# Moving the router's weight and address arithmetic of a decoder layer from VectorE to GpSimd, with the choice of experts made by rank

## The chip, the cores and the metric

The kernel runs on one core of a Trainium2 chip. The metric is the device time of one execution in microseconds; the time before is the median of three executions. The times of single instructions come from one profiled execution, counted from the start of its span. TensorE does the matrix products, VectorE and ScalarE the elementwise work, GpSimd (POOL in the rows) small work and indirect DMAs, SyncE (SP) the other DMAs.

## What is computed

One layer of a decoder for 512 tokens of width 1024 in float32: input projection, block-sparse attention in 8 heads beside a gated linear recurrence in 8 heads, output projection, layer norm, and a hierarchical mixture of 16 experts with a second layer norm. The change touches the router of the mixture:

```python
def hier_moe(x, w_group, b_group, w_expert, b_expert, w_gate, w_up, w_down):
    ...
    g_prob = jax.nn.softmax((xt @ w_group + b_group).astype(jnp.float32), axis=-1)
    g_w, g_idx = lax.top_k(g_prob, 1)
    ...
    e_prob = jax.nn.softmax(e_logits.astype(jnp.float32), axis=-1)
    e_w, e_idx = lax.top_k(e_prob, EXPERT_TOPK)
    e_w = e_w / jnp.sum(e_w, axis=-1, keepdims=True)
    gid = g_idx[:, None] * EXPERTS_PER_GROUP + e_idx
    w_tok = g_w[:, None] * e_w
    ...
    for e in range(N_EXPERTS):
        h = jax.nn.silu(xt @ w_gate[e]) * (xt @ w_up[e])
        y = y + combine[:, e:e + 1] * (h @ w_down[e])
```

Each token has 20 logits: 4 of the groups and 4 experts in each of 4 groups. It takes the best group and in it the two best experts.

## The kernel before

The program is written engine by engine: one instruction list each for SyncE, GpSimd, TensorE, ScalarE and VectorE, kept in step by semaphores. The order in each list is the order in the source, and a waiting instruction holds up all behind it on its engine.

Tokens lie in four tiles of 128 partitions (T = 4). The first half of the program does projection, attention and recurrence; then the output projection, the layer norm and the router; then the experts, one after the other, each on the at most 128 tokens that chose it.

**Products.** Every float32 product is made of three: high part of both, high by low, low by high. ScalarE copies a unit of weights (128 partitions by 2048) from the ring of loaded units to its high part (`ehi(v)`, L1371), VectorE subtracts that from the ring to give the low part (`elo(v)`, L1801). Three such units fit (WBUF = 3). Expert 0 has units 0 to 3 (gate, gate, up, up), expert 1 starts with units 4 and 5. The ring has 12 units of 1 MB, loaded by SyncE (L429).

**Router.** After the layer norm of tile i, TensorE gives its 20 logits, and VectorE puts them into `r_l` (`logits_of`, L1833). When the last tile's are there, `first_max` finds in each group of four the largest and turns it into a one-hot, breaking ties by weights 4, 3, 2, 1 (L1866 to L1870, five instructions); it runs for groups and experts together, and once more for the second expert. The mask of chosen experts (`r_msk`, L1879) goes to TensorE, which counts with two kinds of matmul (L1039, L1041) the place of each token in its expert's list. VectorE turns places into one-hots of slots (`place(e)`, L1895), TensorE multiplies them by token numbers (`placed(e)`, L1048), and VectorE copies the result to `first` (`slots_of`, L1901): the tokens of experts 0 to 3 (EARLY = 4). GpSimd gathers their rows from HBM by it (`gather(e)`, L585); TensorE transposes them (L1118 for expert 0, L1063 for the others).

**Weights and records.** Behind the slots of experts 0 and 1 VectorE makes what later experts need: the differences of logits (L1908 to L1911), which ScalarE takes the exponential of (L1401), the address of each token's record (L1914 to L1918, semaphore `s_addr`), and the weights (L1920 to L1924). GpSimd then scatters eight groups of records to HBM (`scatter_record`, L591), with `gather(2)` behind the fifth and `gather(3)` behind the seventh, reads the full table back (L610) and goes on with the gathers and added rows of the other experts (L617). `gather(2)` fills the buffer that expert 0 used, and the transposes of expert 2 wait for it.

**Fillers.** `keep_warm(n, b)` issues n matmuls on constants whose result nobody reads (L677).

## Time and profile before

| | |
|---|---|
| median of three executions | 617.22 us (616.98 to 617.65) |
| profiled execution, its own time | 616.78 us |
| its span, first to last instruction | 614.9 us |
| TensorE busy | 593.7 us, 97% of the span, 3691 matmuls |
| VectorE busy | 478.1 us, 78% |
| ScalarE busy | 373.9 us, 61% |
| GpSimd busy | 128.2 us, 21%, 111 instructions |
| DMA | 155.77 MB, mean 253 GB/s |

Busy shares are means over the whole program. The chain of waits leads back from the last instruction through whatever released each step; its shares say which engine set the end. A timeline row gives an instruction's start, its duration, and in brackets how long the engine stood idle before it and which engine and line ended that. Row groups that merge equal instructions give a count (x2) and the time from the first's start to the last's end.

### The profile page before, as it was taken

The page shows a single profiled execution, that of the slowest core. Times are in us where ns is not written, and L with a number is a line of the kernel's source. Part 1 is how long each engine was busy: PE and PEld are TensorE (multiplying, and loading weights), DVE is VectorE, ACT ScalarE, POOL GpSimd, SP SyncE. Part 2 cuts the span into 40 slices and gives each one's busy share as a digit, 9 for nine tenths or more (in the row PEclk, how much of TensorE's full clock was granted, in tenths as well). Part 3 has the DMA queues.
Part 4 walks back from the last instruction along what each step waited for, and adds up shares of the span by engine and source line. Part 5 has one row for each costly group of instructions (what it writes and reads, how often), then busy time and mean ns, then how long its engine had stood idle before and what let it go on. Part 6 is the DMA issues. An engine that isn't in the chain of part 4 may idle for free.

```text
span 614.9 us, 9763 instructions
## 1 busy us (share of the span) xinstructions
PE 593.7 (97%) x3691; PEld 478.3 (78%) x3691; DVE 478.1 (78%) x572; ACT 373.9 (61%) x401; POOL 128.2 (21%) x111
## 2 busy tenths in 40 slices
PE   8999999999999999999799999999999999999991
PEld 7878888788888678877688888888888888888880
DVE  3758598794577775446898889888888988888967
ACT  3659434431215984213478877877877777787745
POOL 0004222290000441000484532111110111111010
PEclk9999999999999999999899999999999999999996
DMA  8831233223306002975699999999999999999754
GB/s 325 298 96 60 62 131 114 90 72 78 72 1 205 2 3 102 422 278 225 211 388 419 419 373 366 391 388 394 412 399 390 389 390 388 399 411 395 267 172 136
DMA packets 42573, 155.77 MB, mean 253 GB/s; under 512 B 11955, under 2 KB 12163, under 8 KB 30252
## 3 DMA queue, kind: packets, MB, share of 16 engines
q1 hardware_dynamic: 37516, 138.40, 57.7%
q0 software_dynamic: 5024, 16.92, 10.6%
q8 instruction: 23, 0.38, 0.3%
q14 instruction: 10, 0.08, 0.0%
HBM read 139.96 MB, written 15.34 MB: 253 GB/s over the span
## 4 chain that ended last, share of the span: by engine, by line
PE 92%; DVE 4%; ACT 1%; issue 1%; DMA 1%; DVEq 0%; SPq 0%
PE psum L663 26%; PE psum L665 25%; PE psum L664 25%; PE psum L1063 2%; PE psum L781 2%; PE psum L921 2%; PE psum L898 2%; PE psum L1080 1%; PE psum L885 1%; PE psum L677 1%; DMA cst<-in_c_main 1%; ACT ring L1338 1%; PE psum L823 1%; PE psum L811 1%; PE psum L767 1%
## 5 line engine op out<-in xcount | busy, mean ns | idle before, releaser
L1801 DVE TENSOR_TENSOR w_lo<-ring,w_hi 128x2048 fp32r<-128x2048 f32 x95 | 216.4, 2294 | 23.7 <-ACT w_hi L1371 23.6
L663 PE MATMUL psum<-w_hi,act_hi 128*128 128x512 f32 x538 | 216.5, 402 | 0.8 <-DVE w_lo L1801 0.6
L665 PE MATMUL psum<-w_hi,act_lo 128*128 128x512 f32 x538 | 210.2, 391 | 0.0
L664 PE MATMUL psum<-w_lo,act_hi 128*128 128x512 f32 x538 | 209.9, 390 | 0.0
L1371 ACT ACTIVATE w_hi<-ring 128x2048 fp32r<-128x2048 f32 x96 | 182.1, 1916 | 25.0 <-PE psum L665 22.4
L663 PEld LDWEIGHTS psum<-w_hi,act_hi 128*128 128x128 f32 x538 | 101.2, 188 | 27.0 <-DVE w_lo L1801 4.7
L665 PEld LDWEIGHTS psum<-w_hi,act_lo 128*128 128x128 f32 x538 | 101.0, 188 | 21.8
L664 PEld LDWEIGHTS psum<-w_lo,act_hi 128*128 128x128 f32 x538 | 101.2, 188 | 19.1
L617 POOL DMA_INDIRECT acc_dram<-misc,slots x15 | 25.4, 1693 | 193.7 <-ACT misc L1421 175.9
L1219 ACT ACTIVATE w_hi<-ring 128x2048 fp32r<-128x2048 f32 x17 | 32.6, 1918 | 49.2 <-PE psum L665 47.4
L1530 DVE TENSOR_TENSOR w_lo<-ring,w_hi 128x2048 fp32r<-128x2048 f32 x17 | 39.8, 2344 | 22.3 <-ACT w_hi L1219 22.1
L663 PE MATMUL psum<-act_hi,w_hi 128*128 128x512 f32 x128 | 50.9, 398 | 0.4 <-DVE w_lo L1549 0.4
L664 PE MATMUL psum<-act_lo,w_hi 128*128 128x512 f32 x128 | 49.9, 390 | 0.0
L665 PE MATMUL psum<-act_hi,w_lo 128*128 128x512 f32 x128 | 49.9, 390 | 0.0
L1601 DVE TENSOR_TENSOR misc<-ring 64x256 f32<-64x256 f32 x48 | 34.8, 725 | 1.1
L551 POOL TENSOR_TENSOR ring<-ring 128x2048 f32<-128x2048 f32 x6 | 22.6, 3765 | 54.4 <-PE psum L781 44.8
L575 POOL TENSOR_SCALAR misc<-cst,small 128x64 f32<-128x64 f32 x32 | 14.8, 477 | 80.0 <-DVE small L1732 79.9
L663 PEld LDWEIGHTS psum<-act_hi,w_hi 128*128 128x128 f32 x128 | 24.0, 188 | 6.0 <-issue 0.8
L665 PEld LDWEIGHTS psum<-act_hi,w_lo 128*128 128x128 f32 x128 | 24.0, 188 | 5.1
L664 PEld LDWEIGHTS psum<-act_lo,w_hi 128*128 128x128 f32 x128 | 24.1, 188 | 4.7
L1413 ACT ACTIVATE act_hi<-psum 128x512 fp32r<-128x512 f32 x16 | 9.6, 600 | 25.7 <-PE psum L1080 25.7
L1935 DVE TENSOR_TENSOR act_lo<-psum,act_hi 128x1024 fp32r<-128x1024 f32 x15 | 18.4, 1226 | 7.8 <-ACT act_hi L1405 7.7
(254 smaller groups left out, 697.0 us busy)
## 6 DMA issues: line engine op xcount, KB each, us to landing
ring<-in_w_gate SPq DMA_DIRECT2D x32, 1024.0 KB, 17.3
ring<-in_w_up SPq DMA_DIRECT2D x32, 1024.0 KB, 19.1
ring<-in_w_down SPq DMA_DIRECT2D x32, 1024.0 KB, 19.6
ring<-in_w_in SPq DMA_DIRECT2D x13, 1024.0 KB, 6.2
ring<-in_w_o SPq DMA_DIRECT2D x4, 1024.0 KB, 4.8
acc_dram<-ring SPq DMA_DIRECT2D x5, 512.0 KB, 4.0
ring<-in_x SPq DMA_DIRECT2D x2, 1024.0 KB, 6.5
ring<-strip_dram SPq DMA_DIRECT2D x8, 256.0 KB, 4.7
```

Source lines behind the costliest of these rows:

```text
L551: pool.tensor_tensor(wlev[l].rearrange("p a (n s) -> p (a n) s", s=2 * m), src, src[:, :, m - 1:m].broadcast_to((P, SEQ * PAIRS // (2 * m) ...
L575: pool.tensor_scalar(wide[:, n // (2 * T) % 2, i, 64 * (h % 2):64 * (h % 2) + 64], ones[:, 0:64], prec[:, col:col + 1], None, ALU.mult).th ...
L617: pool.indirect_dma_start(out=acc_dram, out_offset=bass.IndirectOffsetOnAxis(ap=index.bitcast(U32), axis=0), in_=yb[:, b, :], in_offset=No ...
L663: pe.matmul(dst, lh, rh, start=first, stop=False, skip_group_check=True)
L664: pe.matmul(dst, lh, rl, start=False, stop=False, skip_group_check=True)
L665: return pe.matmul(dst, ll, rh, start=False, stop=last, skip_group_check=True)
L1219: act.activation(w_hi[:, u % WBUF, :], ring[:, u % MIX_RING, :], ACT.Copy).then_inc(s_hi, 1)
L1371: act.activation(w_hi[:, v0 % WBUF, :], ring[:, slot, :], ACT.Copy).then_inc(s_hi, 1)
L1530: dve.tensor_tensor(w_lo[:, u % WBUF, :], ring[:, u % MIX_RING, :], w_hi[:, u % WBUF, :].bitcast(F32), ALU.subtract).then_inc(s_lo, 1)
L1601: dve.tensor_tensor(qz[rows, a, :, par, :].rearrange("p c (n t) -> p c n t", t=m), right(wlev[l]), right(hq), ALU.mult).then_inc(s_qz, 1)
L1801: dve.tensor_tensor(w_lo[:, v0 % WBUF, :], ring[:, slot, :], w_hi[:, v0 % WBUF, :].bitcast(F32), ALU.subtract).then_inc(s_lo, 1)
L1935: dve.tensor_tensor(e_lo[:, b, :], banks(0, 2), e_hi[:, b, :].bitcast(F32), ALU.subtract).then_inc(s_etlo, 1)
```

## The change

The five-instruction `first_max`, run twice, is replaced by ranks. `ranks(t0)` subtracts in each four every logit from every other (128 partitions by 160 for two tiles), compares the differences with a table of zeros and smallest numbers that settles ties, and sums: 0 is the largest, 1 the second. For tiles 0 and 1 it stands ahead of the last tile's residual, for tiles 2 and 3 behind the last logits. The mask then takes one comparison and one fused comparison and product.

GpSimd makes the differences, one-hots, addresses and the sum behind the weights, in 25 instructions that each wait for the one before (`then`), where sums over 16 are halved four times (`folded`). VectorE keeps the reciprocal, which now stands behind `place(3)` and ahead of `elo(3)` and waits for `s_addr` 1; one product goes back to GpSimd behind it, ahead of the record scatters. ScalarE's exponential stands behind `ehi(3)`, not behind `ehi(2)`, and waits for GpSimd. `elo(1)` stands right behind `elo(0)`. TensorE's fillers are 29, 9 and 30 instead of 32, 0 and 24, and the first unit's products come in the order high by high, high by low, low by high for all four blocks. The constants have 16 numbers for the ties in place of 4, and the experts' numbers are shifted by 16.

```diff
+            pool.wait_ge(s_rneed, 1)
+            pooled[0] = 4
+            pool.wait_ge(s_pool, 4)
+            then(pool.tensor_tensor(r_x[:, :, 0:NG], r_l[:, :, 0:NG], r_top.broadcast_to((P, T, NG)), ALU.subtract))
+            then(pool.tensor_scalar(r_hot, r_rank[:, :, NG:NL], 0.5, None, ALU.is_lt))
+            then(pool.tensor_scalar(r_hot2, r_rank[:, :, NG:NL], 1.0, None, ALU.is_equal))
+            then(pool.tensor_tensor(four(r_sel[:, 0]), four(r_hot), group_four, ALU.mult))
+            then(pool.tensor_tensor(four(r_sel[:, 1]), four(r_hot2), group_four, ALU.mult))
+            then(pool.tensor_tensor(r_step, r_sel[:, 1], r_sel[:, 0], ALU.subtract))
+            then(pool.tensor_tensor(r_step, r_step, r_l[:, :, NG:NL], ALU.mult))
+            folded(lambda a, b: r_step[:, :, a:b], NE, ALU.add)
+            pool.tensor_copy(r_x[:, :, NG:NG + 1], r_step[:, :, 0:1]).then_inc(s_rneed, 1)
...
+            then(pool.tensor_scalar(r_pos, r_at1, float(NE), None, ALU.mult))
+            then(pool.tensor_tensor(r_pos, r_pos, e16.broadcast_to((P, T, NE)), ALU.add))
+            for k in range(2):
+                then(pool.tensor_tensor(r_sel[:, k], r_sel[:, k], r_pos, ALU.mult))
...
+            folded(lambda a, b: sel[:, :, a:b], NE, ALU.add)
+            then(pool.tensor_copy(addr_i[:, :, :].rearrange("p k i -> p (k i)").rearrange("p (n a) -> p n a", a=1), sel[:, :, 0:1]))
+            pool.wait_ge(s_rexp, 1)
+            folded(lambda a, b: r_x[:, :, a:b], NG, ALU.add)
+            then(pool.tensor_scalar(r_q, r_x[:, :, NG:NG + 1], ALPHA, ALPHA, ALU.mult, ALU.add))
+            pool.tensor_tensor(r_gsum, r_x[:, :, 0:1], r_q, ALU.mult).then_inc(s_addr, 1)
+
             pool.wait_ge(s_pads, 16 * (SEQ // P))
             pool.wait_ge(s_addr, 2)
+            then(pool.tensor_tensor(weight_of(rec_i[:, :, 1, 2:3]), weight_of(rec_i[:, :, 0, 2:3]), r_x[:, :, NG:NG + 1], ALU.mult))
             for n in range(2 * T):
...
-            keep_warm(32, 4)
+            keep_warm(29, 4)
...
             last.then_inc(s_pos, 1)
+            keep_warm(9, 1)
             pe.wait_ge(s_rec, 1)
...
-            keep_warm(24, 1)
+            keep_warm(30, 1)
...
-            act.wait_ge(s_rneed, 1)
-            act.activation(r_x, r_x, ACT.Exp).then_inc(s_rexp, 1)
...
             ehi(3, 0)
+            act.wait_ge(s_rneed, 2)
+            act.activation(r_x, r_x, ACT.Exp).then_inc(s_rexp, 1)
             ehi(4, 0)
...
+            def ranks(t0):
+
+                ls = r_l[:, t0:t0 + 2, :].rearrange("p t (g e) -> p (t g) e", e=4)
+                shape = (P, 2 * (1 + NG), 4, 4)
+                link(dve.tensor_tensor(r_beats, ls.rearrange("p s (a i) -> p s a i", a=1).broadcast_to(shape),
+                                       ls.rearrange("p s (j a) -> p s j a", a=1).broadcast_to(shape), ALU.subtract))
...
+                link(dve.tensor_tensor(r_beats, r_beats, tie.broadcast_to(shape), ALU.is_ge))
+                link(dve.tensor_reduce(r_rank[:, t0:t0 + 2, :].rearrange("p t (g e a) -> p (t g) e a", e=4, a=1), r_beats, AX.X, ALU.add))
+
+            ranks(0)
             residual(T - 1, 1)
...
             link(logits_of(T - 1))
...
-            first_max(r_l, r_hot, r_top, r_first, T * (1 + NG))
...
-            first_max(r_l2, r_hot2, r_top2, r_first2, T * NG)
...
+            ranks(T // 2)
+            link(dve.tensor_scalar(r_group, r_rank[:, :, 0:NG], 0.5, None, ALU.is_lt))
+
+            dve.scalar_tensor_tensor(out=four(r_msk), in0=four(r_rank[:, :, NG:NL]), scalar=1.5, in1=group_four,
+                                     op0=ALU.is_lt, op1=ALU.mult).then_inc(s_mask, 1)
...
             elo(0, 0)
+            elo(1, 0)
...
-            elo(1, 0)
             elo(2, 0)
             place(2)
             place(3)
+            dve.wait_ge(s_addr, 1)
+            dve.reciprocal(weight_of(rec_i[:, :, 0, 2:3]), r_gsum).then_inc(s_addr, 1)
             elo(3, 0)
```

The order of the instructions on VectorE, from the slots of experts 0 and 1 (`first`) to the fourth unit's low part, before. L1801 is `elo`, L1895 `place`, L1960 and L1962 the low part of expert 0's rows:

```order
L1901 CAST first<-psum 128x2 x2
L1908 TENSOR_TENSOR misc<-misc 128x4x4
L1909 TENSOR_TENSOR misc<-misc 128x16
...
L1923 RECIPROCAL rec_i<-misc 128x4
L1924 TENSOR_TENSOR rec_i<-rec_i,misc 128x4
L1801 TENSOR_TENSOR w_lo<-ring,w_hi 128x2048
L1960 TENSOR_TENSOR act_lo<-psum,act_hi 128x512
L1962 TENSOR_TENSOR act_lo<-psum,act_hi 128x512
L1801 TENSOR_TENSOR w_lo<-ring,w_hi 128x2048 x2
L1895 TENSOR_TENSOR act_hi<-cst,misc 128x512
L1895 TENSOR_TENSOR act_lo<-cst,misc 128x512
L1801 TENSOR_TENSOR w_lo<-ring,w_hi 128x2048
```

And now, with the line numbers of the changed kernel (L1848 is `elo`, L1934 `place`):

```order
L1940 CAST first<-psum 128x2 x2
L1848 TENSOR_TENSOR w_lo<-ring,w_hi 128x2048 x2
L1982 TENSOR_TENSOR act_lo<-psum,act_hi 128x512
L1984 TENSOR_TENSOR act_lo<-psum,act_hi 128x512
L1848 TENSOR_TENSOR w_lo<-ring,w_hi 128x2048
L1934 TENSOR_TENSOR act_hi<-cst,misc 128x512
L1934 TENSOR_TENSOR act_lo<-cst,misc 128x512
L1989 RECIPROCAL rec_i<-misc 128x4
L1848 TENSOR_TENSOR w_lo<-ring,w_hi 128x2048
```

The small instructions are gone, the second unit's low part stands ahead of expert 0's rows, and the reciprocal stands ahead of the fourth unit's.

On GpSimd, from the gathers of experts 0 and 1 to those of 2 and 3, before:

```order
L585 DMA misc<-x_dram,first 128x1024 x2
L591 DMA slot_dram<-rec_i,addr_i 8192x3 x5
L585 DMA misc<-x_dram,first 128x1024
L591 DMA slot_dram<-rec_i,addr_i 8192x3 x2
L585 DMA misc<-x_dram,first 128x1024
```

And now (L589 is the gather, L595 the scatter, L616 a halving):

```order
L589 DMA misc<-x_dram,first 128x1024 x2
L621 TENSOR_TENSOR misc<-misc 128x4x4
L622 TENSOR_SCALAR misc<-misc 128x64
...
L629 COPY misc<-misc 128x4
L632 TENSOR_SCALAR misc<-misc 128x64
...
L638 CAST addr_i<-misc 128x8
...
L642 TENSOR_TENSOR misc<-misc 128x4
L646 TENSOR_TENSOR rec_i<-rec_i,misc 128x4
L595 DMA slot_dram<-rec_i,addr_i 8192x3 x5
L589 DMA misc<-x_dram,first 128x1024
```

26 instructions stand between the second gather and the first scatter, and the third gather is still behind five scatters.

## Rows read from the trace of the kernel before

**Rows 1.** The page, part 4: chain of waits, shares by engine.

```profile
PE 92%; DVE 4%; ACT 1%; issue 1%; DMA 1%; DVEq 0%; SPq 0%
```

**Rows 2.** Timeline of TensorE, 285 to 350: start us, us, instruction, tile, count [idle before].

```profile
290.67 3.65 PE L677 MATMUL psum<-cst 128*128 128x256 bf16 x32
295.88 0.25 PE L1039 MATMUL psum<-msk_b,ones_b 128*128 128x64 bf16 x4 [1.56 <-DVE msk_b L1879]
...
298.37 4.46 PE L677 MATMUL psum<-cst 128*128 128x256 bf16 x24
302.67 1.16 PE L1118 MATMUL psum<-cst,misc 128*128 128x128 f32 x8
...
307.69 0.47 PE L663 MATMUL psum<-w_hi,act_hi 128*128 128x512 f32 x1 [0.59 <-DVE w_lo L1801]
...
329.67 1.04 PE L1063 MATMUL psum<-cst,misc 128*128 128x128 f32 x8
```

**Rows 3.** Busy time by stretch: us, PE, PEld, DVE, ACT, POOL; granted clock; DMA.

```profile
299.00:300.00 1.00, 1.00 (x6) 0.70 (x5) 0.90 (x6) 0.22 (x1) 0.70 (x2) 0.50 0.00 0
```

**Rows 4.** Timeline of VectorE, 285 to 350.

```profile
287.51 0.69 DVE L1820 SCALAR_TENSOR_TENSOR ring<-ring,psum 128x512 f32<-128x512 f32 x1 [3.89 <-PE psum L665]
...
292.34 0.24 DVE L1866 TENSOR_REDUCE misc<-misc 128x20 f32<-128x80 f32 x1
...
295.51 0.22 DVE L1879 TENSOR_TENSOR msk_b<-misc 128x64 bf16<-128x64 f32 x1
...
301.53 2.29 DVE L1801 TENSOR_TENSOR w_lo<-ring,w_hi 128x2048 fp32r<-128x2048 f32 x1
...
305.26 4.48 DVE L1801 TENSOR_TENSOR w_lo<-ring,w_hi 128x2048 fp32r<-128x2048 f32 x2
...
310.86 2.29 DVE L1801 TENSOR_TENSOR w_lo<-ring,w_hi 128x2048 fp32r<-128x2048 f32 x1
...
315.23 2.29 DVE L1801 TENSOR_TENSOR w_lo<-ring,w_hi 128x2048 fp32r<-128x2048 f32 x1
```

**Rows 5.** Line 585 (row gather) alone, 298 to 299: issue to landing.

```profile
DMA to landing us min/median/max: 4.2/4.2/4.2
```

**Rows 6.** Line 442 (last quarter written to HBM) alone, 291 to 293.

```profile
L442 SPq DMA_DIRECT2D x_dram<-ring x1: 320/320/320, 292.2 to 292.2; - x1
...
DMA to landing us min/median/max: 2.9/2.9/2.9
```

**Rows 7.** Timeline of GpSimd, 285 to 400: gathers (L585) and record scatters (L591).

```profile
298.45 1.05 POOL L585 DMA_INDIRECT misc<-x_dram,first  x1 [64.55 <-DVE first L1901]
...
302.47 2.24 POOL L591 DMA_INDIRECT slot_dram<-rec_i,addr_i  x1 [1.69 <-DVE rec_i L1924]
305.01 0.98 POOL L591 DMA_INDIRECT slot_dram<-rec_i,addr_i  x1 [0.30 <-issue]
...
310.89 3.10 POOL L591 DMA_INDIRECT slot_dram<-rec_i,addr_i  x1 [0.30 <-issue]
315.58 2.79 POOL L585 DMA_INDIRECT misc<-x_dram,first  x1 [1.59 <-DVE first L1901]
```

**Rows 8.** Timeline of GpSimd, small operations elsewhere in the program.

```profile
135.67 0.39 POOL L560 CAST rec_i<-cst 128x24 int32<-128x24 f32 x1
136.00 0.29 POOL L561 CAST tri_b<-cst 128x128 bf16<-128x128 f32 x1
...
341.90 0.18 POOL L614 COPY small<-slots 128x1 f32<-128x1 f32 x1 [5.49 <-DMA slots<-slot_dram]
```

**Rows 9.** The page, part 5: GpSimd operation on 64 elements, the nearest in size.

```profile
L575 POOL TENSOR_SCALAR misc<-cst,small 128x64 f32<-128x64 f32 x32 | 14.8, 477 | 80.0 <-DVE small L1732 79.9
```

**Rows 10.** Timeline of ScalarE, 285 to 360.

```profile
295.78 1.28 ACT L1401 ACT_TABLE_LOAD   x1
...
307.19 1.92 ACT L1371 ACTIVATE w_hi<-ring 128x2048 fp32r<-128x2048 f32 x1 [2.68 <-PE psum L1129]
```

**Rows 11.** Line 585 alone, 315 to 316: issue to landing.

```profile
DMA to landing us min/median/max: 10.6/10.6/10.6
```

More of the change, by code:

```diff
@@ L66 @@
 C_SCAN = C_MASK + 64 * (1 + len(LEVELS))
-C_W4 = C_SCAN + SEQ
-C_E16 = C_W4 + 4
+C_TIE = C_SCAN + SEQ
+C_E16 = C_TIE + 16
 C_REC = C_E16 + NE
@@ L87, in shape_constants @@
     c[:, C_SCAN:C_SCAN + SEQ] = (np.arange(SEQ) % CH != 0)[None]
-    c[:, C_W4:C_W4 + 4] = [4, 3, 2, 1]
-    c[:, C_E16:C_E16 + NE] = np.arange(NE)
+    c[:, C_TIE:C_TIE + 16] = [0 if i < j else np.finfo(np.float32).tiny for j in range(4) for i in range(4)]
+    c[:, C_E16:C_E16 + NE] = np.arange(NE) - NE
     for i in range(T):
@@ L297, in build, with four @@
         r_msk = msk_b[:, :].rearrange("p (i e) -> p i e", i=T)
-        r_l, r_hot, r_top, r_first = rcol(T, NL), rcol(T, NL), rcol(T * (1 + NG), 1), rcol(T * (1 + NG), 1)
-        r_l2, r_hot2, r_top2, r_first2 = rcol(T, NE), rcol(T, NE), rcol(T * NG, 1), rcol(T * NG, 1)
-        r_x, r_d, r_both, r_gsum, r_gw, r_q = rcol(T, NG + 1), rcol(T, NG), rcol(T, NE), rcol(T, 1), rcol(T, 1), rcol(T, 1)
+        r_l, r_group, r_hot, r_hot2, r_top = rcol(T, NL), rcol(T, NG), rcol(T, NE), rcol(T, NE), rcol(T, 1)
+        r_rank, r_beats, r_step = rcol(T, NL), rcol(2 * (1 + NG), 4, 4), rcol(T, NE)
+        r_x, r_gsum, r_q = rcol(T, NG + 1), rcol(T, 1), rcol(T, 1)
+        def four(v):
+            return v.rearrange("p t (g e) -> p t g e", g=NG)
+        group_four = r_group.rearrange("p t (g a) -> p t g a", a=1).broadcast_to((P, T, NG, EPG))
         r_sel, r_pos, r_t16, r_at1, r_adr, r_cnt = rcol(2, T, NE), rcol(T, NE), rcol(2 * T, NE), rcol(T, NE), rcol(2 * T, 1), rcol(1)
@@ L598, in _, with then, folded @@
             gather(1)
+            pooled = [2]
+            def then(ins):
+                pooled[0] += 1
+                ins.then_inc(s_pool, 1)
+                pool.wait_ge(s_pool, pooled[0])
+            def folded(v, n, op):
+                while n > 1:
+                    n //= 2
+                    then(pool.tensor_tensor(v(0, n), v(0, n), v(n, 2 * n), op))
+            pool.wait_ge(s_rneed, 1)
+            pooled[0] = 4
+            pool.wait_ge(s_pool, 4)
+            then(pool.tensor_tensor(r_x[:, :, 0:NG], r_l[:, :, 0:NG], r_top.broadcast_to((P, T, NG)), ALU.subtract))
@@ new lines, in _ @@
+            folded(lambda a, b: r_step[:, :, a:b], NE, ALU.add)
+            pool.tensor_copy(r_x[:, :, NG:NG + 1], r_step[:, :, 0:1]).then_inc(s_rneed, 1)
+            e16 = cst[:, C_E16:C_E16 + NE].rearrange("p (a e) -> p a e", a=1)
+            then(pool.tensor_scalar(r_pos, r_at1, float(NE), None, ALU.mult))
+            then(pool.tensor_tensor(r_pos, r_pos, e16.broadcast_to((P, T, NE)), ALU.add))
+            for k in range(2):
+                then(pool.tensor_tensor(r_sel[:, k], r_sel[:, k], r_pos, ALU.mult))
@@ new lines, in _ @@
+            sel = r_sel.rearrange("p k i e -> p (k i) e")
+            folded(lambda a, b: sel[:, :, a:b], NE, ALU.add)
[4 more added lines that the diff above has]
+            pool.tensor_tensor(r_gsum, r_x[:, :, 0:1], r_q, ALU.mult).then_inc(s_addr, 1)
@@ L1120, in _ @@
             pe.wait_ge(s_x1tsb, T + 2)
-            pe.wait_ge(s_lo, MIX_UNITS + 1)
-            block = lambda k: (slice(k * P, (k + 1) * P), slice(k * DE, (k + 1) * DE))
-            for k in range(4):
-                xs, ws = block(k)
-                high(bank(2), e_hi[:, 0, xs], w_hi[:, 0, ws], w_lo[:, 0, ws], k == 0)
-            pe.wait_ge(s_xtlofirst, 1)
-            for k in range(4):
-                xs, ws = block(k)
-                last = pe.matmul(bank(2), e_lo[:, 0, xs], w_hi[:, 0, ws], start=False, stop=False, skip_group_check=True)
+            pe.wait_ge(s_hi, MIX_UNITS + 1)
+            passes = [(e_hi, w_hi), (e_hi, w_lo), (e_lo, w_hi)]
+            for n, (x, w) in enumerate(passes):
+                if n == 1:
+                    pe.wait_ge(s_lo, MIX_UNITS + 1)
+                elif n == 2:
+                    pe.wait_ge(s_xtlofirst, 1)
+                for k in range(4):
+                    last = pe.matmul(bank(2), x[:, 0, k * P:(k + 1) * P], w[:, 0, k * DE:(k + 1) * DE], start=(n == 0 and k == 0), stop=False,
+                                     skip_group_check=True)
             last.then_inc(s_used, 1)
@@ L1885, in _ @@
             dve.wait_ge(s_mask, 1)
+            dve.tensor_reduce(r_top, r_l[:, :, 0:NG], AX.X, ALU.max)
             dve.wait_ge(s_pos, 1)
             pos = psum[:, 7, 0:T * NE].rearrange("p (i e) -> p i e", i=T)
-            e16 = cst[:, C_E16:C_E16 + NE].rearrange("p (a e) -> p a e", a=1)
-            link(dve.scalar_tensor_tensor(out=r_at1, in0=pos, scalar=1.0, in1=r_msk, op0=ALU.add, op1=ALU.mult))
+            dve.scalar_tensor_tensor(out=r_at1, in0=pos, scalar=1.0, in1=r_msk, op0=ALU.add, op1=ALU.mult).then_inc(s_rneed, 1)
+            dve.wait_ge(s_rneed, 1)
             def place(e):
```

36 lines of the change are left out of this document (1 added, 35 removed).

## The prediction

> **What bounds the kernel now.** I read the chain of waits first: TensorE carries 92% of the span [rows 1]. In the expert half it never starves for long; the largest holes are around the router, where a token's choice of experts must become an index before the first rows can be gathered. The timeline of TensorE shows them [rows 2]: it waits 1.56 us for the choice mask (295.88), fills time with 24 dummy matmuls (298.37, 4.46 us), transposes expert 0's rows at 302.67, waits 0.59 us for the low part of the second weight unit (307.69), and transposes expert 2's rows at 329.67. From there on the experts run on TensorE's own pace. So a change here is worth what it moves the transpose at 329.67, if nothing behind it is hurt. The 24 dummies are slow: 32 others took 3.65 us (114 ns each), these 186 ns each, since the granted clock is 0.50 at 299 to 300 [rows 2, 3], the lower level (1.2 GHz), after TensorE had done little since the first dummies ended at 294.3.
>
> **The choice.** VectorE starts twelve instructions in a row at 292.34 and the mask at 295.51 [rows 4]: 3.17 us, 0.264 each. The change leaves three on 160 elements, one on 16, and the mask. From 0.24 us for 80 elements and 2.29 for 2048 [rows 4] an element costs 1.04 ns, so 160 cost 0.32, with the 0.03 between starts 0.35; three are 1.05, the small one 0.2. The mask starts at 293.6 instead of 295.5: **1.9 us earlier**. The same three for tokens 0 to 255 lie ahead of the wait for TensorE that ends at 287.51 after 3.89 us idle [rows 4], which covers their 1.05; without it they would cost 1.05.
>
> **TensorE's fillers.** 29 dummies from 290.67 last 3.3 us, to 294.0, when the mask's matmuls can start. Nine more (1.0 us) bridge to the one-hot matmuls. The clock should not fall, so the 30 dummies ahead of expert 0 last 3.4 us, from 296.5 to 299.9. Expert 0's gather started at 298.45, released by VectorE's slots [rows 7], and landed 4.2 later [rows 5], just as the old dummies ended. It moves to 296.55. The HBM rows that it reads were issued at 292.2 and landed 2.9 later [rows 6], so they don't hold it. It lands at 300.75: the transposes come 1.9 earlier. The new order of the twelve first products (four with low weights moved behind four with high) issues as many matmuls: nothing, since both low parts are there by then.
>
> **Low weights.** VectorE loses 15 small instructions between the slots and 301.53 and runs two low-part subtractions there instead of one, so the 0.59 wait at 307.69 goes [rows 2]: 0.6 more. Together 2.5 us; at best the transpose of 329.67 would come at 327.2.
>
> **What GpSimd takes over.** 25 instructions in one chain, each waiting for the one before, until the first weight sum (s_addr 1), and one product after VectorE's reciprocal. Nothing in the trace is such a chain. The nearest rows: a copy of one element 0.18 and two casts that start 0.33 apart [rows 8], and 0.44 to 0.48 for 64 elements with an operand per partition [rows 9]. Bounds are 0.18 and 0.44 per step; I take 0.33, as most steps have 4 to 64 elements. GpSimd also yields to VectorE. A record scatter takes 0.98 (305.01), but 2.24 when it starts inside the subtraction of 301.53 to 303.82, and 3.10 inside that of 310.86 to 313.15 [rows 4, 7]: both end 0.85 to 0.9 behind the subtraction's end. So a GpSimd instruction issued into a subtraction of two SBUF tensors waits for its end. The Trainium skill (SBUF — State Buffer, Who interferes with whom) says the same, that such an instruction and a GpSimd one that reads SBUF exclude each other for the whole instruction; but by it the first to issue wins, so a GpSimd step would also hold a subtraction up, by at most its 0.3. The trace has no case that I could price.
> By these rows: the second gather waits for the first subtraction (right behind the slots, 296.7 to 299.0) and ends at 299.9; the chain starts at 301.3 behind the second. Until the third (from 305.26, less 1.9: 303.4 to 305.7) some 6 steps pass, 3 at the edges of it and of the two one-hots, to 307.0. There VectorE waits for the chain and leaves GpSimd alone: 16 steps of 0.33 end at **312.3** (bounds 309.4 and 314.5; the lower one is set by ScalarE, below).
> The Trainium skill (GPSIMD Engine Reference, Engine selection) advises VectorE for such elementwise work, GpSimd being about twice slower for two inputs. By it a 0.2 us step would be 0.4, and the chain end at 313.8; that is inside the bounds.
>
> **The exponential.** ScalarE's copy at 307.19 moves to 305.3, ends at 307.2, then comes the table load of 1.28 [rows 10] and the exponential, 308.6 at the earliest; the last four steps of GpSimd's chain follow it. The 12 steps that it waits for are then done (9 by 307.0, three more by 308.0). Its next copy is held up 0.3, which VectorE's wait covers.
>
> **VectorE waits, first effect.** Behind the new wait stand the low part of the fourth unit, expert 1's low part, the slots of experts 2 and 3, and the low part of the fifth. Before, the fourth ran at 310.86 and the fifth at 315.23 to 317.52 [rows 4], just ahead of TensorE. Now the fourth starts at 312.6, ends at 314.9; with the same distance at most (2.1) or the work alone (1.4) the fifth ends at 318.6 to 319.3: TensorE would be 1.1 to 1.8 us later than before, take 1.4.
>
> **GpSimd's queue, second effect, and the larger one.** The eight record scatters and the gather of expert 2, which stands behind five of them, are queued behind the chain. Before, the scatters started at 302.47, the fifth ended at 313.99, and the gather started at 315.58 [rows 7]. Now: wait at 312.3, reciprocal, then the last product, which meets the fourth subtraction and waits until 314.9; scatters from 315.3. Five took 11.5 us where each met a subtraction, and would take 6.4 alone (0.98 and 0.30 between); VectorE has rather fewer subtractions per us in that stretch, so I take 10. The gather starts at 325.6, **10.0 later** (bounds: 318.7 and 329.2). It needed 10.6 us to land [rows 11], since the weight loads fill the DMA engines, against 4.2 on an idle queue [rows 5]. It lands at 336.2. Before, it landed at 326.2 and was needed at 329.67: slack of 3.5. So TensorE transposes expert 2 at 336.2, **6.5 later than before**; this swallows both the 2.5 won and the 1.4 lost. In a wait of over 4 us the clock should fall again: the old fall cost 4.46 less 24 times 0.114, or 1.7 us [rows 2]; bounds 0 and 1.7, I take 0.9, as I don't know how much falls into the wait itself.
> Sum: 6.5 and 0.9 make 7.4. The profiled execution took 616.78, 0.44 under the median 617.22. On the median: **624.6**.
>
> **Rivals.**
> *A, VectorE's wait alone.* The gather lands in time because it moves faster, and only the first effect stays: 617.2 and 1.4, 618.6 (617.0 to 619.2). For it: a gather on an idle queue takes 4.2. Against: the loads are just as dense there.
> *B, faster.* GpSimd's steps cost under 0.2, the scatters slip between subtractions (6.4), and the gather started at 318.7 lands, even after 8.5 us, before 327.2: then 2.5 are won, 614.7, less up to 0.5 of the fifth unit's low part. It decides at a gather start of about 317 with 10.6 to land, or 323 with 4.2. For it: the exponential is due just as the steps would then be done. Against: even with free steps the last product meets the fourth subtraction, and scatters did meet one each.
> *C, the queue is later still.* The slots' table, read behind all eight scatters, is late for expert 1's output weight and for the added rows, and ScalarE waits too: 629 or more. Before, it came in at 341.9 [rows 8]; 10 us later is near what the next output can stand.
> *That the choice does not shorten*: the ranks' broadcasts could run slower, up to 0.5 each; this takes 0.5 from the 1.9 and nothing from the forecast, since the gather of expert 2 sets it.
>
> **How the numbers follow.** Forecast 0.60, its own range 620.5 to 628.5 (gather start 2.5 us either way, clock 0 to 1.7); A 0.13, half of it within 0.2% (1.2 us, about what a measurement tells from no change); B 0.17; C 0.10. Faster 0.17, same 0.06, slower 0.77. The range from 615.0 to 628.5 leaves out C and half of B.
>
> **What would show it.** The mask at 293.6; no 0.50 clock at 299; GpSimd's chain from 301 to about 312 with VectorE idle before the reciprocal; the gather of expert 2 starting near 325 and TensorE idle over 4 us ahead of expert 2's transposes. I am wrong if that gather lands before TensorE asks for it, or if the chain is done by 309.

## The result and the profile after

Before 617.1 us (median of four executions, 616.85 to 617.65), changed 624.18 us (median of four, 623.39 to 628.72); ratio 1.0124, 95% interval 1.0098 to 1.0149. The changed kernel is slower by 1.2%. The forecast was 624.6. The median of 624.18 lies between 623.42 and 624.94, and the four executions spread over 5.3 us. The changed kernel's profiled execution took 623.39 with a span of 621.6, against 616.78 and 614.9: 6.7 us more of span.

TensorE's share of the chain of waits fell from 92 to 88% [rows 1], and GpSimd's, not among the shares before, is 4%:

```profile
PE 88%; DVE 4%; POOL 4%; issue 2%; DMA 1%; ACT 0%; DVEq 0%; POOLq 0%
```

The chain itself, from 312 to 338 us (start, us, what), is the view that settles where the time went. It leaves TensorE and runs through GpSimd's queue:

```profile
312.34 0.21 POOL misc L642
...
312.58 0.19 DVE rec_i L1989
...
312.90 2.12 POOL rec_i L646
...
315.31 0.07 POOL slot_dram L595
...
316.70 2.50 POOL slot_dram L595
...
323.44 2.23 POOL slot_dram L595
...
325.97 8.36 DMA misc<-x_dram,first
...
334.37 1.97 PE psum L1109 x8
```

GpSimd's last sum (L642), VectorE's reciprocal (L1989), the product that waits inside a subtraction (L646, 2.1 us), five record scatters (L595, from 315.31 to 325.67; three are shown), the gather of expert 2 in flight for 8.4 us, and only then TensorE's transposes at 334.37, where they stood at 329.67 before [rows 2].

TensorE, timeline, 285 to 350:

```profile
290.88 3.33 PE L722 MATMUL psum<-cst 128*128 128x256 bf16 x29
...
296.61 3.45 PE L722 MATMUL psum<-cst 128*128 128x256 bf16 x30
300.99 1.16 PE L1164 MATMUL psum<-cst,misc 128*128 128x128 f32 x8 [0.93 <-DMA misc<-x_dram,first]
...
307.97 1.04 PE L1109 MATMUL psum<-cst,misc 128*128 128x128 f32 x8
...
315.00 0.79 PE L708 MATMUL psum<-w_hi,act_hi 128*128 128x512 f32 x1 [2.45 <-DVE w_lo L1848]
...
334.37 1.97 PE L1109 MATMUL psum<-cst,misc 128*128 128x128 f32 x8 [2.31 <-DMA misc<-x_dram,first]
```

The front works as meant. The whole execution is 0.2 us later when the router begins. The 30 dummies take 3.45 us (115 ns each) where 24 took 4.46, expert 0's transposes come at 300.99 instead of 302.67, and expert 1's at 307.97 instead of 310.53. At the fourth unit TensorE waits 2.45 us, at expert 2 2.31 us.

VectorE, timeline, 285 to 350:

```profile
287.72 0.69 DVE L1867 SCALAR_TENSOR_TENSOR ring<-ring,psum 128x512 f32<-128x512 f32 x1 [2.82 <-PE psum L710]
...
293.83 0.22 DVE L1920 SCALAR_TENSOR_TENSOR msk_b<-misc 128x64 bf16<-128x64 f32 x1
...
303.58 2.28 DVE L1848 TENSOR_TENSOR w_lo<-ring,w_hi 128x2048 fp32r<-128x2048 f32 x1
305.78 0.81 DVE L1934 TENSOR_TENSOR act_hi<-cst,misc 128x512 fp32r<-128x512 f32 x1
...
312.58 0.18 DVE L1989 RECIPROCAL rec_i<-misc 128x4 f32<-128x4 f32 x1 [5.33 <-POOL misc L642]
312.67 2.28 DVE L1848 TENSOR_TENSOR w_lo<-ring,w_hi 128x2048 fp32r<-128x2048 f32 x1
...
322.54 2.29 DVE L1848 TENSOR_TENSOR w_lo<-ring,w_hi 128x2048 fp32r<-128x2048 f32 x1 [0.91 <-ACT w_hi L1418]
```

The wait that ended at 287.51 after 3.89 us idle [rows 4] is now 2.82: the ranks of the first two tiles lie in it. The mask starts at 293.83. Before the reciprocal at 312.58 VectorE stands idle for 5.33 us, and the fourth subtraction (L1848) follows it, and then the fifth at 316.07.

GpSimd, timeline, some of the 25 steps:

```profile
303.23 0.33 POOL L626 TENSOR_TENSOR misc<-misc 128x64 f32<-128x64 f32 x1
303.63 2.42 POOL L627 TENSOR_TENSOR misc<-misc 128x64 f32<-128x64 f32 x1
306.12 1.77 POOL L616 TENSOR_TENSOR misc<-misc 128x32 f32<-128x32 f32 x4
...
309.91 1.23 POOL L616 TENSOR_TENSOR misc<-misc 128x64 f32<-128x64 f32 x4
...
312.90 2.11 POOL L646 TENSOR_TENSOR rec_i<-rec_i,misc 128x4 f32<-128x4 f32 x1 [0.36 <-DVE rec_i L1989]
```

The step at 303.23 takes 0.33 us; the next, the same operation on the same size, takes 2.42, since it starts inside the subtraction of 303.58 to 305.86. The four halvings at 306.12 beside the one-hots take 1.77, those at 309.91 with VectorE idle 1.23.

ScalarE, timeline: the exponential comes as early as its table load lets it.

```profile
307.44 1.28 ACT L1497 ACT_TABLE_LOAD   x1
308.73 0.22 ACT L1497 ACTIVATE misc<-misc 128x20 f32<-128x20 f32 x1
```

Granted clock by stretch (us; busy PE, PEld, DVE, ACT, POOL; clock; DMA share, GB/s):

```profile
296.00:300.00 4.00, 4.00 (x36) 3.45 (x36) 3.46 (x5) 0.00 (x0) 3.01 (x2) 1.00 0.72 256
314.00:320.00 6.00, 5.00 (x12) 3.93 (x13) 5.93 (x8) 1.38 (x1) 5.10 (x4) 0.50 1.00 422
334.00:338.00 4.00, 3.63 (x13) 3.27 (x14) 0.56 (x1) 1.62 (x2) 1.52 (x2) 0.57 0.99 405
```

At 296 to 300 the clock is full; before, it was 0.50 at 299 to 300 [rows 3]. It is 0.50 from 314 to 320, from within the wait at the fourth unit on, and again for much of 334 to 338, behind the wait for expert 2's rows.

### The profile page after: what moved, and what is told of

The parts are those of the page before. It is cut to its first block, busy times and chain, and to the rows that moved or that the text cites. A ratio compares the mean times of both kernels' runs of the same rounds, so it can differ in the third digit from the quotient of the medians.

```text
span 621.6 us, 9796 instructions
## 1 busy us (share of the span) xinstructions
PE 598.1 (96%) x3703; PEld 482.6 (78%) x3703; DVE 475.8 (77%) x554; ACT 374.0 (60%) x401; POOL 137.7 (22%) x137
## 4 chain that ended last, share of the span: by engine, by line
PE 88%; DVE 4%; POOL 4%; issue 2%; DMA 1%; ACT 0%; DVEq 0%; POOLq 0%
PE psum L708 24%; PE psum L710 23%; PE psum L709 23%; PE psum L1109 2%; PE psum L826 2%; PE psum L943 2%; PE psum L966 2%; PE psum L722 2%; PE psum L930 2%; DMA misc<-x_dram,first 1%; POOL slot_dram L595 1%; PE psum L1126 1%; PE psum L868 1%; PE psum L856 1%; PE psum L1003 1%
## 5 line engine op out<-in xcount | busy, mean ns | idle before, releaser
L1848 DVE TENSOR_TENSOR w_lo<-ring,w_hi 128x2048 fp32r<-128x2048 f32 x95 | 216.9, 2298 | 25.2 <-ACT w_hi L1418 23.9
```

The costliest lines, as they stand in the source:

```text
L1848: dve.tensor_tensor(w_lo[:, v0 % WBUF, :], ring[:, slot, :], w_hi[:, v0 % WBUF, :].bitcast(F32), ALU.subtract).then_inc(s_lo, 1)
```

## The experiments

Two theories stood against each other. **The queue:** the records and, behind five of them, expert 2's gather leave GpSimd too late; all else is swallowed by TensorE's wait for that gather. **The wait:** VectorE's idle time ahead of the reciprocal, with the half clock behind it, is what costs. Each run is compared with executions of the kernel before on the same chip, whose medians were 617.32 to 617.77 us; so two runs are compared by their ratios, not by their times.

**1. The gather second in the queue.**

```diff
             for n in range(2 * T):
-                if n == 5:
+                if n == 1:
                     pool.wait_ge(s_slots, 3)
                     gather(2)
```

> The changed kernel with the gather of expert 2 behind the first record scatter instead of the fifth. Queue theory (the gather's place in GpSimd's queue sets TensorE's restart at expert 2): the gather starts near 316.7 us, lands by 327, TensorE no longer waits for it (2.3 us) and its clock does not fall a second time (1.7 us): 4.0 us faster than the changed kernel, about 620. Rival (VectorE's wait for GpSimd's sum, with the half clock behind it, is all that costs): no change, 623.4 to 624.2.

Measured: 622.37 us, ratio 1.0091 (1.0061 to 1.0122); 620.69 in the profiled execution. The gather started at 316.27 and TensorE's wait at expert 2 was gone (transposes at 330.43), but only some 2 us of 4 came back: the ratio fell from 1.0124 to 1.0091, with intervals that overlap, so that the profile says more here than the time. GpSimd's and ScalarE's timelines show why:

```profile
316.27 2.51 POOL L589 DMA_INDIRECT misc<-x_dram,first  x1 [0.30 <-issue]
...
348.67 1.50 POOL L659 COPY small<-slots 128x1 f32<-128x1 f32 x1 [5.03 <-DMA slots<-slot_dram]
```

```profile
350.26 1.12 ACT L1466 ACTIVATE misc<-psum,small 128x1024 f32<-128x1024 f32 x1 [2.47 <-POOL small L659]
```

The table of records, read back behind all eight scatters, gives expert 1's output weight (L659). It came at 348.67, ScalarE's output (L1466) waited 2.47 us for it, and TensorE 1.61 behind that. The gather was the first thing to be late; the table is the next.

**2. The same, and TensorE kept busy at the fourth unit.**

```diff
+            keep_warm(22, 4)
             in_unit(3, 0, 1, 3, 0)
             step(1, 0)
```

> As the run before, and 22 dummy matmuls on TensorE ahead of expert 0's fourth unit, where it waits for VectorE. If the 0.50 clock from 313.9 to 320.7 us comes from that wait, it is gone, and a further 2.8 us (half of the 5.7 us that TensorE works in it): about 617. If the clock falls for another reason: as the run before, about 620.

Measured: 622.42 us, ratio 1.0067 (1.0048 to 1.0086). The 22 dummies ran in 2.58 us and the granted clock is 1.00 over 312 to 322, so the half clock at 314 to 320 goes with the idle time at the fourth unit; that such idle time does not always bring it is seen in run 9, where TensorE waited 2.63 us and kept the full clock. The time was not that of the expectation, 617, but that of run 1:

```profile
312.54 2.58 PE L722 MATMUL psum<-cst 128*128 128x256 bf16 x22
```

```profile
ACT misc L1467 <- POOL small L659: 4.0, 1, 4.0
...
PE psum L708 <- DVE w_lo L1849: 3.1, 1, 3.1
```

(the second fence: engine and line waited for, us in total, times, longest.) Little was won in front. In run 1 the lower clock lasted only 3.4 us, a loss of 1.7 and not of 2.8; here TensorE waited 0.6 us for VectorE right behind (at 318.59 and 321.78), this execution began its router 0.5 us later, and expert 2's transposes came at 330.56, against 330.43 in run 1. Of the ten scatters and gathers ahead of the table one more took over 1.8 us, the ten took 2.9 us longer in all, the table came at 351.64, 3 us later than in run 1, and TensorE waited 3.1 us in one go behind it. The little that was won in front was more than paid at the table.

**3. Rank alone.** The weights and addresses go back to VectorE, to their old place; ranks, fillers and the order of the first unit's products stay.

```diff
-            then(pool.tensor_tensor(r_x[:, :, 0:NG], r_l[:, :, 0:NG], r_top.broadcast_to((P, T, NG)), ALU.subtract))
...
+            link(dve.tensor_tensor(r_x[:, :, 0:NG], r_l[:, :, 0:NG], r_top.broadcast_to((P, T, NG)), ALU.subtract))
+            dve.tensor_scalar(r_hot, r_rank[:, :, NG:NL], 0.5, None, ALU.is_lt)
...
             elo(0, 0)
-            elo(1, 0)
```

> Only the choice by rank and the fillers are kept: weights and addresses are made on VectorE again, where they were before, 17 instructions, and the exponential stands where it was. Queue theory: gather of expert 2 in time, mask 1.9 us earlier, low part of the second unit late by up to 0.9: 615 to 615.7, faster than before by 1.5 to 2. Rival (the ranks or fillers themselves cost): 617 or more.

Measured: 615.67 us (ten executions), ratio 0.9968 (0.9958 to 0.9978): faster than both kernels. TensorE's timeline:

```profile
301.37 1.16 PE L1123 MATMUL psum<-cst,misc 128*128 128x128 f32 x8 [1.39 <-DMA misc<-x_dram,first]
...
306.39 0.47 PE L667 MATMUL psum<-w_hi,act_hi 128*128 128x512 f32 x1 [0.60 <-DVE w_lo L1807]
...
328.37 1.04 PE L1068 MATMUL psum<-cst,misc 128*128 128x128 f32 x8
```

Transposes of expert 0 at 301.37 and of expert 2 at 328.37, the wait for the second unit's low part still there at 0.60. So the choice by rank does what it says, and the loss comes with the move to GpSimd and the order on VectorE that goes with it. The two profiled executions differ by 0.8 us of span only (614.1 against 614.9); where the rest of the 2 us between the medians lies is not shown. A repetition beside other runs (eleventh run):

> The run with rank alone and weights on VectorE once more, beside the other two on one chip: 615.7, 0.2 to 0.4% under the kernel before.

gave 615.66, ratio 0.9972 (0.9960 to 0.9984).

**4. The mechanism alone, in the kernel before.** Nothing of the change; only the two gathers behind all scatters.

```diff
             for n in range(2 * T):
-                if n == 5:
-                    pool.wait_ge(s_slots, 3)
-                    gather(2)
                 if n == 7:
-                    gather(3)
+                    pool.wait_ge(s_slots, 3)
                 scatter_record(n)
+            gather(2)
+            gather(3)
```

> The kernel before with the gathers of experts 2 and 3 behind all eight record scatters; nothing else. Queue theory: the gather of expert 2 starts near 321.5 us instead of 315.6, lands near 332, TensorE waits 2.4 us for it and may lose up to 1.7 at half clock: 619.5 to 621. Rival (a late gather is made good by an emptier queue or by slack): 617.1, no change.

Measured: 621.05 us, ratio 1.0048 (1.0031 to 1.0065). GpSimd's first scatter and gather, and TensorE's transposes:

```profile
303.60 2.23 POOL L591 DMA_INDIRECT slot_dram<-rec_i,addr_i  x1 [1.88 <-DVE rec_i L1923]
...
322.92 2.51 POOL L585 DMA_INDIRECT misc<-x_dram,first  x1 [0.30 <-issue]
```

```profile
333.03 1.16 PE L1062 MATMUL psum<-cst,misc 128*128 128x128 f32 x8 [1.64 <-DMA misc<-x_dram,first]
```

The gather started at 322.92, TensorE waited 1.64 us for it. Late gathers alone make the kernel slower, by 3 us (0.48%). The profiled execution is longer than that of before by 4.7 us of span, and not all of this is the gather: expert 1's transposes, which stand ahead of it, came 1.6 us late already (312.10 against 310.53), as this execution had the lower clock from 297 to 305 (before: 298 to 302). Another 1.8 arise by expert 2's transposes, and 1.1 by those of expert 3.

**5. The old fillers in the changed kernel.**

```diff
-            keep_warm(29, 4)
+            keep_warm(32, 4)
...
-            keep_warm(9, 1)
...
-            keep_warm(30, 1)
+            keep_warm(24, 1)
```

> The changed kernel with TensorE's fillers as before (32, none, 24). Queue theory: the front of the router is swallowed by the wait for expert 2's gather, so nothing changes in the time (within 0.5 us of the changed kernel, 4 to 7 above the kernel before), though the clock is 0.50 near 297 to 300 us again. Rival (the fillers win or cost something in the end): a difference over 1 us.

Measured: 628.62 us, ratio 1.0164 (1.0107 to 1.0220), the four executions 623.33, 627.90, 629.33 and 630.41. The expectation failed as to the size, though the interval overlaps that of the changed kernel (1.0098 to 1.0149), so that a cost of the old fillers is not shown. It failed as to the clock, too: the 24 fillers took 2.79 us at the full clock. The profile shows how fine the balance is. The chain on GpSimd and the first three scatters stand where they do in the changed kernel, to 0.1 us. Then:

```profile
315.31 1.08 POOL L595 DMA_INDIRECT slot_dram<-rec_i,addr_i  x1 [0.29 <-POOL rec_i L646]
...
322.16 2.62 POOL L595 DMA_INDIRECT slot_dram<-rec_i,addr_i  x1 [0.31 <-issue]
...
326.35 2.13 POOL L589 DMA_INDIRECT misc<-x_dram,first  x1 [0.30 <-issue]
```

The fourth scatter met a subtraction (2.62 us, against 0.96 in the changed kernel), so did the gather (2.13 against 1.00). It landed at 336.6, 2.3 later, TensorE waited 5.64 us, and there the clock was at its lower level for 6.8 us instead of 3.4. What tipped it was the start of one subtraction on VectorE:

```profile
321.66 2.29 DVE L1847 TENSOR_TENSOR w_lo<-ring,w_hi 128x2048 fp32r<-128x2048 f32 x1
```

In the changed kernel it started at 322.54, behind 0.91 us of waiting for ScalarE and 0.4 us behind the start of the fourth scatter; here it started 0.5 us ahead of the scatter, with no wait before it. The likely reason is that the lower clock at the fourth unit lasted 3.4 us here and 6.8 there, so that TensorE gave ScalarE and VectorE their next work sooner. The changed kernel's own executions spread over 5 us in the same way. That each of them is such a slip is argued from these two profiles, not shown.

**6. VectorE's wait moved back.**

```diff
-            dve.wait_ge(s_addr, 1)
-            dve.reciprocal(weight_of(rec_i[:, :, 0, 2:3]), r_gsum).then_inc(s_addr, 1)
             elo(3, 0)
             xt_lo(1, 1)
             slots_of(2, EARLY, 6)
             elo(4, 0)
+            dve.wait_ge(s_addr, 1)
+            dve.reciprocal(weight_of(rec_i[:, :, 0, 2:3]), r_gsum).then_inc(s_addr, 1)
```

> The changed kernel with VectorE's wait and reciprocal behind the fifth unit's low part instead of ahead of the fourth's. VectorE no longer idles over 5 us, TensorE no longer waits 2.45 us at the fourth unit. Queue theory: the scatters start at most 0.8 us later, so the gather of expert 2 lands at 334.5 to 335.5 all the same and the time is that of the changed kernel, 623.5 to 625. Rival (VectorE's wait costs by itself): 2 to 4 us faster than the changed kernel.

Measured: 630.74 us, ratio 1.0214 (1.0197 to 1.0231): **slower** than the changed kernel by 6 us, though TensorE's wait at the fourth unit was gone. It waited 1.28 us for the fifth unit instead, kept the full clock up to there, and was ready for expert 2 at 328.54, 3.5 us sooner than in the changed kernel (332.06). That was all lost in the wait for the gather, 11.3 us: the wait theory is dead as an account of the time. The queue theory is right on what sets the time, but had expected no later gather. GpSimd's timeline:

```profile
317.19 2.71 POOL L595 DMA_INDIRECT slot_dram<-rec_i,addr_i  x1 [0.55 <-POOL rec_i L646]
...
328.56 2.42 POOL L595 DMA_INDIRECT slot_dram<-rec_i,addr_i  x1 [0.30 <-issue]
331.29 1.00 POOL L589 DMA_INDIRECT misc<-x_dram,first  x1 [0.30 <-issue]
```

Five scatters took from 317.19 to 330.98, 13.8 us, where they took 10.4 in the changed kernel: VectorE is idle for only 0.9 us in all between 317 and 330, and each of the five takes over 2 us. They also began 1.9 us later, not 0.8 as expected: GpSimd's four halvings met the fourth subtraction, which now ran beside them (3.69 us, against 1.77), and the last product waited 2.4 us for the reciprocal. The gather started 5.3 us later than in the changed kernel, expert 2's transposes came at 339.81, and the clock stayed low long after (second and third column of numbers: us and TensorE busy):

```profile
332.00:340.00 8.00, 0.20 (x1) 0.20 (x2) 0.00 (x0) 0.00 (x0) 4.19 (x5) 0.51 1.00 408
340.00:346.00 6.00, 6.00 (x19) 5.04 (x19) 2.56 (x2) 2.82 (x2) 2.35 (x4) 0.51 0.06 17
```

From 339.8 to 345.9 TensorE worked at half clock, a loss of 3.0 us; with the 10.1 us by which the transposes are late that makes 13.1 of the 13.2 us of span over the kernel before.

**7. Both waits taken out.** The reciprocal as in run 6, and expert 2's gather ahead of all scatters.

```diff
+            pool.wait_ge(s_slots, 3)
+            gather(2)
             pool.wait_ge(s_pads, 16 * (SEQ // P))
             pool.wait_ge(s_addr, 2)
...
-                if n == 5:
-                    pool.wait_ge(s_slots, 3)
-                    gather(2)
```

> The reciprocal behind the fifth unit's low part and the gather of expert 2 ahead of all record scatters. Both waits of the changed kernel are gone, expert 2's transposes come at 327 to 327.5 us. If the records' table is the third in the row: it comes at 348 to 349 us, 3 us after TensorE's pace would need expert 1's weight, and ScalarE's output of expert 1 waits for it; with the clock's fall 618.5 to 620.5. If nothing else is late: 615.

Measured: 625.53 us, ratio 1.0121 (1.0101 to 1.0140). TensorE did not wait for expert 2's rows, but reached them at 330.08 and not at 327: it waited 1.28 us for the fifth unit, and in this execution the first 29 fillers took 4.99 us instead of 3.33, at the lower clock for the most part. And the table took over as the bound, by more than expected: it came at 353.85.

```profile
PE psum L707 <- DVE w_lo L1847: 7.1, 2, 5.8
...
ACT misc L1465 <- POOL small L658: 6.7, 1, 6.7
```

ScalarE waited 6.7 us for GpSimd's weight, TensorE 5.8 us in one go behind it. The table comes 7 to 13 us later than with rank alone (341.0 in run 3, 347.8 in the changed kernel, 353.9 here): in these runs, moving work about in the queue only chose who is late.

**8. Rank alone with the old fillers.**

> The run with rank alone and weights on VectorE, with TensorE's fillers as before (32, none, 24). If only the choice wins the time: the 24 slow fillers (4.5 us from 296.6) end at 301, as the gather lands at 300.8, and the time is that of rank alone, 615.7. If the clock kept up by the new fillers is part of it: about 1 us slower, 616.5 or more.

(the edit is that of run 5, on the kernel of run 3.) Measured: 616.68 us (ten executions, 615.52 to 617.79), ratio 0.9986 (0.9976 to 0.9997), against 0.9968 with the new fillers (0.9958 to 0.9978, so that the intervals just touch). Its profiled execution took 615.68, as fast as run 3's, and the 24 fillers ran at the full clock, 2.79 us, with TensorE idle for 1.13 and 1.49 us around them. So in this execution, as in run 5, the earlier mask alone kept the clock up, without the nine fillers between. What the slower half of its executions did no profile shows. By the medians the fillers are worth about 1 us, and how stays open.

**9. The last product on VectorE.**

```diff
-            dve.reciprocal(weight_of(rec_i[:, :, 0, 2:3]), r_gsum).then_inc(s_addr, 1)
+            link(dve.reciprocal(weight_of(rec_i[:, :, 0, 2:3]), r_gsum))
+            dve.tensor_tensor(weight_of(rec_i[:, :, 1, 2:3]), weight_of(rec_i[:, :, 0, 2:3]), r_x[:, :, NG:NG + 1], ALU.mult).then_inc(s_addr, 1)
```

> The changed kernel with the last product on VectorE behind the reciprocal, so that GpSimd's queue holds nothing but scatters when the sum is done. The product ran 2.1 us on GpSimd, of which 1.9 was the fourth subtraction. If the block by subtractions sets the queue, the first scatter now meets the same subtraction: it ends near 316.0 instead of 316.4 us, and the time stays within 1.5 us of the changed kernel (622.5 to 625.5). If the product itself was the cost: expert 2's gather 2 us earlier, 620 to 621.

Measured: 626.73 us, ratio 1.0134 (1.0114 to 1.0154). The time is above the expected stretch, but the ratio cannot be told from the changed kernel's 1.0124 (1.0098 to 1.0149). That the product was the cost, 620 to 621, is refuted. The first scatter met the fourth subtraction as foreseen (ended at 316.00), and each of the next four took over 2 us, too:

```profile
313.70 2.30 POOL L595 DMA_INDIRECT slot_dram<-rec_i,addr_i  x1 [1.28 <-DVE rec_i L1989]
...
325.06 3.06 POOL L595 DMA_INDIRECT slot_dram<-rec_i,addr_i  x1 [0.30 <-issue]
328.43 2.07 POOL L589 DMA_INDIRECT misc<-x_dram,first  x1 [0.30 <-issue]
```

Five took 14.4 us and the gather started at 328.43. In this execution the clock did not fall at the fourth unit, and VectorE's subtractions came closer together: one started at 321.64, with no wait before it. In the changed kernel the same one waited 0.91 us for ScalarE and started at 322.54, and one scatter slipped through. The reading, argued from these profiles and that of run 5, is that the loss on TensorE paid a part of itself back on GpSimd.

**10. Rank alone, weights later.** To take the 0.60 us left in run 3, the first subtraction goes ahead of the address chain and the five weight instructions behind the second; expert 2's gather goes out behind three scatters instead of five.

```diff
             for n in range(2 * T):
-                if n == 5:
+                if n == 3:
...
+            elo(0, 0)
             link(dve.tensor_tensor(r_x[:, :, 0:NG], r_l[:, :, 0:NG], r_top.broadcast_to((P, T, NG)), ALU.subtract))
...
-            dve.wait_ge(s_rexp, 1)
-            link(dve.tensor_reduce(r_gsum, r_x[:, :, 0:NG], AX.X, ALU.add))
...
-            elo(0, 0)
...
             elo(1, 0)
+            dve.wait_ge(s_rexp, 1)
+            link(dve.tensor_reduce(r_gsum, r_x[:, :, 0:NG], AX.X, ALU.add))
...
```

> Rank alone with weights on VectorE, but the first subtraction ahead of the address chain, the five weight instructions behind the second subtraction, and expert 2's gather behind three scatters. It takes the 0.60 us wait for the second unit's low part. If the records' table has the slack that the trace shows (it is read at 341.0 us, needed at 346.5), it gains 0.6 us on rank alone. If scatters that start 5 us later make the table late again: 1 to 3 us slower than rank alone.

Measured: 616.79 us, ratio 0.9989 (0.9975 to 1.0002). The wait for the second unit's low part stayed, at 0.59. In that order the second subtraction (at 304.97, 2.28 us) stands behind expert 0's two low parts, the last of which starts at 304.37, and VectorE even stood idle for 0.61 us ahead of them: it is not a full VectorE that TensorE waits for there, but this order. The table came at 346.01, 5 us later than in run 3, 1 of which this execution had lost by expert 1's transposes. The median shows no gain, and run 3 stays the best version. What the profiled execution lost, it lost ahead of the edit: its first 29 fillers ran at the lower clock for the most part,

```profile
290.80 4.99 PE L681 MATMUL psum<-cst 128*128 128x256 bf16 x29
```

4.99 us for the 29 against 3.33 in run 3. From expert 1's transposes to the end it took 304.6 us, run 3 304.9. So the later table cost nothing in it, and whether the slower median comes from the edit or from more executions with such a start is not shown.

## Why the prediction was right

The time forecast was 624.6 and is 624.18; the mechanism and nearly every time up to the gather's start are those of the forecast: GpSimd's chain holds up its queue, the gather of expert 2 starts 10 us late, TensorE waits for it, and both what was won in front and what the fourth unit cost are swallowed. That the time agrees within 0.4 us is luck. Two terms behind the gather's start are off by 1.8 and 0.8 us and partly cancel, the profiled execution lies 0.8 under the median, and the executions spread over more than 5 us. Step by step, predicted and measured on the profiled execution:

| step | predicted | measured |
|---|---|---|
| mask starts | 293.6 | 293.83, with all 0.2 later |
| expert 0's transposes | 300.8 | 300.99 |
| won up to expert 1's transposes | 2.5 us | 2.56 us |
| exponential | 308.6 | 308.73 |
| GpSimd's sum done | 312.3 | 312.54 |
| first scatter | 315.3 | 315.31 |
| five scatters | 10 us | 10.4 us |
| expert 2's gather starts | 325.6 | 325.97 |
| it lands | 336.2 | 334.33 |
| expert 2's transposes, later by | 6.5 us | 4.7 us |
| half clock behind them | 0.9 us | 1.7 us |
| TensorE idle ahead of expert 2 | over 4 us | 2.31 us |
| span, longer by | 7.4 us | 6.7 us |

Two terms were mis-sized against each other. **The landing:** taken as 10.6 us from its issue [rows 11], it was 8.4. The gather of [rows 11] itself took 2.79 us on GpSimd, as it started inside a subtraction [rows 4, 7]; the new one took 1.00, which accounts for 1.8 of the 2.2 us. I had carried that block over into a place where I had not looked whether a subtraction stood. **The clock:** I took half of 1.7 us; the 3.4 us at the lower level began as TensorE resumed (334.4), so all of it was paid. The 4.7 and 1.7 us make 6.4 of the 6.7 of span; the other 0.3 is not traced.

**One sign did not come.** The prediction named TensorE idle over 4 us ahead of expert 2's transposes. It was 2.31, because the gather landed 1.9 us earlier than forecast and TensorE itself came 1.0 later than the 331.1 that the forecast implies (329.67 and 1.4).

**A second fall was missed.** The wait at the fourth unit was foreseen, its clock was not: TensorE worked at half speed from 315.0 to 320.7, 2.8 us. Rival A, priced at 1.4, would have been 2.4: TensorE stood ready for expert 2 at 332.06, against 329.67. It added nothing to the time at expert 2, as the gather came later still, which is what run 6 confirms from the other side.

**The clock in front.** The prediction put the full clock of the 30 fillers down to the fillers ahead of them. Runs 5 and 8 had it without them, so the earlier mask, which left TensorE less idle time, was enough in their profiled executions.

**The steps of GpSimd.** 0.33 was the estimate; 24 steps from 301.53 to 312.54, less 2.1 us in which one stood inside a subtraction and 0.5 beside the one-hots, make 0.35 each. (The prediction's working by a step of 0.4 us, 307.0 and 16 steps, gives 313.4 and not 313.8. Its range, by the terms it names, would be 621.2 to 627.9, a little narrower than stated. Neither touches the forecast.) The rule of the Trainium skill (SBUF — State Buffer, Who interferes with whom), that a VectorE instruction with two SBUF inputs and a GpSimd one that reads SBUF exclude each other, agrees with the trace in one direction: the step of 2.42 us above. In the other it fits VectorE's one-hots, which took 0.81 and 0.74 beside GpSimd's steps against 0.69 and 0.68 before; this direction, which the trace of before could not price, is worth 0.18 us in all. The Trainium skill's advice to give elementwise work on a tile to VectorE and not to GpSimd (GPSIMD Engine Reference, Engine selection) holds in this case by the runs with rank alone against the changed kernel. The reason that the Trainium skill gives there is about twice the time for an instruction with two inputs. Here 0.35 us a step stand against 0.20 on VectorE (run 3, 17 instructions from 296.78 to 300.26). But the queue matters more. 25 steps are 9 us where VectorE needs 3.5, and they sit ahead of a queue that was already the tightest thing in the router.

**Rival C** (the table late) was given 0.10 as a case beyond the forecast. It did not bind in the changed kernel, where the table came at 347.8 and ScalarE wanted it at 354.0; of these 6.2 us of slack 4.0 are the wait for the gather and the clock behind it. It bound in runs 1, 2 and 7. **Rival B** (faster) needed a gather start of 317; run 1 had 316.27 and was still not faster. TensorE reached expert 2 at 330.43 and not at 327.2, because of the wait at the fourth unit and the clock behind it, and lost more to the table behind that, which is C. B's price, 614.7, ought to have named both as conditions.

## What to carry to other kernels

Work that goes to an idle engine goes into that engine's queue: look first at what stands behind it there and when each is needed, not at how idle the engine is. When the first late thing in a queue is cured, ask for the next one at once; here gather, then table, each hid the other. And an engine that is blocked by another's instructions gets its throughput from that one's idle time, so that removing a wait elsewhere can make it slower, as run 6 did.

## What had not been expected of the hardware

GpSimd's indirect DMAs depend on VectorE's pace: five scatters took 10.4 us, 13.8 and 14.4 us in three kernels that differ only in where the reciprocal and the last product stand (the changed kernel, runs 6 and 9); each takes 0.96 to 1.09 us alone and up to 3.06 when it starts inside one of VectorE's subtractions. A kernel so balanced spreads: 623.3 to 630.4 us for one program in run 5. The granted clock did not follow the length of a wait by any rule seen here. After the wait of about 2.5 us at the fourth unit its lower level (1.2 GHz) was granted for 6.8 us in the changed kernel, for 3.4 in runs 1 and 5, and not at all in run 9; after the 2.3 us wait for expert 2 in the changed kernel for 3.4, around 5.6 us in run 5 and 7.3 us in run 9 for 6.8, and around 11.3 us in run 6 for 13.7, beginning at times within the wait and at times only when TensorE had resumed.

The clock also differed between executions with the same instructions ahead of it: the first 29 fillers took 3.33 us in most profiled executions, and 4.99 in those of runs 7 and 10, where the granted clock was at its lower level from 291.0 to 294.4 and from 291.3 to 294.7. The table's landing depended on how much the weight loads still moved: from GpSimd's issue to landing it took 5.2 us in the changed kernel (224 GB/s in the 3 us from 342), and 2.0 in run 6, where the long wait had let the loads stop (8 GB/s). So in runs 5, 6 and 9 the table came at 344.1 to 345.2, sooner than in the changed kernel, though the gather was later.
